# Interleaving the two key/value groups in the compression products of the sparse mixer

## What is computed

```python
HEAD_DIM, NSA_KV_GROUPS, CMP_BLOCK, CMP_STRIDE, CMP_HIDDEN = 64, 4, 32, 16, 128

def compress_blocks(tok, pe, w1, w2):
    seq = tok.shape[1]
    n_cmp = (seq - CMP_BLOCK) // CMP_STRIDE + 1
    idx = np.arange(n_cmp)[:, None] * CMP_STRIDE + np.arange(CMP_BLOCK)[None, :]
    blk = tok[:, idx] + jnp.transpose(pe, (1, 0, 2))[None, None]
    hid = jax.nn.gelu(jnp.einsum('bclgd,gldh->bgch', blk, w1))
    return jnp.einsum('bgch,ghd->bgcd', hid, w2)

def nsa_mixer(...):
    ...
    k_cmp = compress_blocks(rope(kv[:, :, 0]), pe_k, w1_k, w2_k)
    v_cmp = compress_blocks(kv[:, :, 1], pe_v, w1_v, w2_v)
    ...
```

## Time and profile before

| | us |
|---|---|
| median of 3 runs | 4570.61 |
| lowest and highest run | 4568.33, 4572.18 |
| the profiled execution | 4559.27 |
| its span in the profile | 4558.0 |
| PE busy in the span | 4293.0 (94%) |
| the compression, first to last matmul | 2352.80 to 2428.3 |

### The profile page before, as it was taken

How to read it: one execution, slowest core, us unless ns; L and a number is a source line. 1 busy time by engine, 2 the same in 40 slices (tenths; PEclk the granted TensorE clock), 3 DMA queues, 4 the chain that set the end, 5 groups by cost and what they waited for, 6 DMA issues and landing times.

```text
span 4558.0 us, 71840 instructions
## 1 busy us (share of the span) xinstructions
PE 4293.0 (94%) x30760; PEld 3958.4 (87%) x30760; DVE 3061.0 (67%) x4411; ACT 1964.3 (43%) x2499; POOL 117.0 (3%) x112
## 2 busy tenths in 40 slices
PE   7989999999998999979888899999999899999998
PEld 6878888787886888868786899999998799999998
DVE  6667675675767866457535699845955689954864
ACT  4445454454534544445324443243244544234233
POOL 0000000000003000020000000000000000000000
PEclk9989999899999999979975999999999999999999
DMA  5533545254541545415431354354254345345344
GB/s 198 185 108 136 189 176 186 89 185 159 187 163 47 194 176 185 158 46 193 144 114 46 121 182 152 112 185 167 103 186 148 114 173 181 108 159 185 120 158 148
DMA packets 94701, 679.29 MB, mean 149 GB/s; under 512 B 11296, under 2 KB 11952, under 8 KB 12848
## 3 DMA queue, kind: packets, MB, share of 16 engines
q1 hardware_dynamic: 91152, 662.74, 40.5%
q0 software_dynamic: 1024, 7.61, 0.4%
q10 hardware_dynamic: 2208, 4.34, 0.3%
HBM read 671.48 MB, written 3.17 MB: 148 GB/s over the span
## 4 chain that ended last, share of the span: by engine, by line
PE 82%; DVE 14%; ACT 2%; issue 1%; DMA 0%; POOL 0%; ACTq 0%; DVEq 0%; SPq 0%; POOLq 0%
PE psum L625 21%; PE psum L554 15%; PE psum L556 14%; PE psum L555 14%; PE psum L626 10%; PE psum L1185 3%; DVE slab_low L1627 2%; DVE room L2261 1%; DVE room L1898 1%; DVE x L1749 1%; DVE room L2277 1%; DVE room L2259 1%; DVE room L2263 1%; PE psum L576 1%; DVE room L1788 1%
## 5 line engine op out<-in xcount | busy, mean ns | idle before, releaser
L1627 DVE TENSOR_TENSOR slab_low<-slab,slab_high 128x2048 fp32r<-128x2048 f32 x632 | 1448.0, 2291 | 791.0 <-ACT slab_high L1204 788.6
L1204 ACT ACTIVATE slab_high<-slab 128x2048 fp32r<-128x2048 f32 x632 | 1204.0, 1905 | 530.4 <-PE psum L626 258.0
L554 PE MATMUL psum<-h_parts,slab_high 128*128 128x256 f32 x3424 | 994.4, 290 | 66.2 <-DVE h_parts L1672 61.6
L625 PE MATMUL psum<-h_parts,slab_high 128*128 128x512 f32 x2816 | 996.2, 398 | 40.2 <-DVE h_parts L1962 35.5
L555 PE MATMUL psum<-h_parts,slab_high 128*128 128x256 f32 x3424 | 979.7, 286 | 0.0
L556 PE MATMUL psum<-h_parts,slab_low 128*128 128x256 f32 x3424 | 979.1, 286 | 0.0
L626 PE MATMUL psum<-h_parts,slab_low 128*128 128x256 f32 x2816 | 790.6, 281 | 0.0
L554 PEld LDWEIGHTS psum<-h_parts,slab_high 128*128 128x128 f32 x3424 | 667.9, 195 | 79.4 <-issue 70.1
L625 PEld LDWEIGHTS psum<-h_parts,slab_high 128*128 128x128 f32 x2816 | 531.7, 189 | 173.7 <-issue 28.3
L555 PEld LDWEIGHTS psum<-h_parts,slab_high 128*128 128x128 f32 x3424 | 668.5, 195 | 2.0 <-issue 1.9
L556 PEld LDWEIGHTS psum<-h_parts,slab_low 128*128 128x128 f32 x3424 | 667.6, 195 | 0.0
(11 more groups left out here) (291 smaller groups left out, 4766.7 us busy)
## 6 DMA issues: line engine op xcount, KB each, us to landing
slab<-in_up SPq DMA_DIRECT2D x176, 1024.0 KB, 4.8
slab<-in_keys_up SPq DMA_DIRECT2D x128, 1024.0 KB, 4.8
slab<-in_keys_down SPq DMA_DIRECT2D x128, 1024.0 KB, 4.8
slab<-in_down SPq DMA_DIRECT2D x88, 1024.0 KB, 4.8
slab<-in_w_in SPq DMA_DIRECT2D x16, 1024.0 KB, 4.8
slab<-in_wq SPq DMA_DIRECT2D x16, 1024.0 KB, 4.9
slab<-in_w_pw SPq DMA_DIRECT2D x12, 1024.0 KB, 4.8
slab<-in_w_qkv SPq DMA_DIRECT2D x12, 1024.0 KB, 4.8
```

Source lines behind the costliest of these rows:

```text
L554: nc.tensor.matmul(out, lhs[0], rhs[0], start=first, stop=False, **options)
L625: nc.tensor.matmul(out, lhs[0], rhs, start=first, stop=False, **options)
L1204: nc.scalar.activation(k.high[m % PARTS][:, 0:width], k.slabs[m % RING][:, 0:width], ACT.Copy).then_inc(k.rounded.up())
L1627: nc.vector.tensor_tensor(k.low[m % RING][:, 0:width], k.slabs[m % RING][:, 0:width], k.high[m % PARTS][:, 0:width], ALU.subtract).then_in ...
```

## The change

The loop over the two row halves (`gg`) moves from outside the steps to the innermost place: each of the three matmuls of a step is issued for `gg` = 0 and right behind it for `gg` = 1. The same 768 matmuls with the same operands, banks and sums are issued; each bank still gets its 48 terms per slab in the same order. `product` is no longer called here; the matmuls now stand on L1052.

```diff
-                    for gg in range(2):
-                        rows = slice(HD * gg, HD * gg + HD)
-                        out = k.banks[gg][0:NCMP, (2 * a + g) * P:(2 * a + g + 1) * P]
-                        for n in range(16):
-                            cols, at = slice(n * P, (n + 1) * P), 16 * half + n
-                            flat = v.parted_flat[a]
-                            mm = self.product(out, (flat[rows, g, at, 0:NCMP], flat[rows, g, at, NCMP:2 * NCMP]),
-                                              (high[rows, cols], low[rows, cols]), half == 0 and n == 0, half == 1 and n == 15)
+                    for n in range(16):
+                        cols, at = slice(n * P, (n + 1) * P), 16 * half + n
+                        first, last = half == 0 and n == 0, half == 1 and n == 15
+                        flat = v.parted_flat[a]
+
+                        for m, (s, part) in enumerate(((0, high), (0, low), (1, high))):
+                            for gg in range(2):
+                                rows = slice(HD * gg, HD * gg + HD)
+                                mm = nc.tensor.matmul(k.banks[gg][0:NCMP, (2 * a + g) * P:(2 * a + g + 1) * P],
+                                                      flat[rows, g, at, s * NCMP:(s + 1) * NCMP], part[rows, cols],
+                                                      start=first and m == 0, stop=last and m == 2)
                     mm.then_inc(k.slab_done.up())
```

## The result

The changed kernel ran at 4535.74 us in the median of 4 runs (4522.99 to 4543.10), the kernel before at 4569.47 (4566.75 to 4572.18). The ratio is 0.9923 with a 95% interval of 0.9899 to 0.9947: 35 us faster, 24 to 46. The forecast was 4522.3 with a range of 4516 to 4540. The time lies inside, 13 us above the forecast. It also lies within 1 us of the 4536.3 that rival (a), the lower clock throughout, gave; so the time alone does not tell the forecast's case from that rival, and the profile has to.

The account below looks back on a forecast made before the run. PE alone was taken to bound the compression stage (75.5 us at clock 0.50). Pairing, upper clock and slab feed together gave minus 48.3 us: 4559.27 to 4511.0 profiled, 4522.3 with the 11.3 us offset; range 4516 to 4540.

Parts of the forecast that it names:

- rival (a): Compression stage: the clock stays at 0.50, only the pairing counts, minus 34.3 us, 4536.3 us; chance 0.31.
- Pairs side by side: First term, compression matmuls on PE: both row halves overlap throughout, 41.0 us at the lower clock for 75.5, minus 34.3.
- The clock: Second term, compression stage: with all rows fed PE's clock rises to 1.00 at 2358; a slab takes 2.7 us, not 9.4.
- The feed: Slab loads, ACT and DVE limit the faster stage: PE waits 1.5 us for slab 4; L1513 starts 48.3 us sooner.
- rival (d): Upper clock comes, but slab feed is worse or clock falls back: 3 to 8 us less gain; 0.62 including the main case.
- Behind the stage: Copy, gelu, second layer and attention move as one with the stage; attention's clock worth 2 us either way.
- The median: Median of the runs lies 11.3 us above the profiled execution; the same offset turns 4511.0 into 4522.3.
- (b): Overlap at a row-half switch is only a draining store, so nothing changes: 4570 within a few us; chance 0.04.
- (c): Changing row half every matmul empties the array, each costs 305 ns: 159 us more, 4730; chance 0.03.

Follow-up runs that it names:

- strips of 32 rows: Changed kernel with each compression matmul reading only the lower 32 of its 64 rows; 4542.29 us, ratio 0.9931 to the kernel before.
- the block of 12: Row half changes after every 12 matmuls (four steps) instead of after each matmul; run once, 4541.11 us.
- the repeat: The changed kernel again, nothing edited, with more rounds; 4530.72 us in the median of 6 runs, ratio 0.9906 to the kernel before.
- the two kernels with other row counts: Changed kernel with 32 of 64 rows read per matmul (4542.29 us), and with one matmul over all 128 rows per pair (4529.31 us).
- the block of 3: Row half changes after each step of three matmuls instead of after each matmul; 4535.17 us, ratio 0.9911 to the kernel before.
- all rows in one matmul: Changed kernel with one matmul over all 128 rows in place of each pair, 384 in the stage; 4529.31 us, ratio 0.9899 to the kernel before.
- the warm start: Changed kernel with 30 full-size products of no use ahead of the stage, where PE waits; 4523.99 us, ratio 0.9889 to the kernel before.
- the last two kernels: Both on 30 useless products ahead of the stage: ACT's last two roundings and DVE's rests moved later (4523.69 us); 64 more useless products behind the stage (4531.93 us).
- the fillers: Changed kernel with 30 useless products ahead of the stage and 64 more behind it where PE waits; 4531.93 us, ratio 0.9905 to the kernel before.

## Why the prediction was right, point by point

- **Pairs side by side.** Forecast 384 pairs at 107 ns and 34.3 us for this term. Measured alone, with strips of 32 rows, the stage took 41.2 us to the copy, which is 34.3 us less. The reading of the earlier trace rows as a rule was right, and the block of 12 gives its reach, some four matmuls. Two details of it were off without changing the sum: by the line numbers the two streams are 2357.45, .56, .66 and 2357.46, .54, .65, and the last matmul of L1084 at the lower clock took 0.42 us where 0.47 was estimated, which makes 50 ns for one and not 49.
- **The clock.** Forecast a rise at 2358 for a start at 2352.8, by fed rows. It rose 5.0 us after the start (2366.2 for 2361.2), 4.8 in the repeat (2358.2 for 2353.4), and the two kernels with other row counts show that it went by the rows. The choice against rival (a) was the one that mattered for the mechanism; the rows of L1084 and L999 carried it. For the number it mattered little: the range held both cases.
- **The feed.** Forecast 27.2 us from first matmul to copy; it was 30.0 and 29.7. The step that was mis-sized is the sum at the upper clock. A pair takes 60 ns and not 56 (2.9 us a slab, near the upper end of the bounds given), and so does one matmul for all rows, so it is not the pairing that costs the 4 ns; loads take longer when two are in flight, 4.8 to 5.8 us, where 4.8 had been taken as fixed; and there are the pauses for instructions, which the prediction didn't have at all. Slab 9's load began 22.7 us in (forecast 20.4) and ACT took it up at 28.2 (forecast 25.2). The list of DMA issues of the changed kernel has, from 2366 to 2386 us (count, KB, median us to landing):

```profile
slab<-in_w SPq DMA_DIRECT2D x4, 1024.0 KB, 5.2
slab<-in_w_nsa_out SPq DMA_DIRECT2D x2, 1024.0 KB, 5.2
```

  Slab 4's start came out at the time forecast (14.7 us in, measured 14.65), in part by luck. Its rest was ready when the sum had it, but the forecast's wait of 1.5 us for it was not there: a pause for instructions of 1.0 us and the slower pace had used it up (in the repeat PE waited 0.25 us). It is the slabs behind it that lost 3 us, slab 4 itself 1.9 in one pause. That is rival (d), of which the cause was named only in part.
- **Behind the stage.** From the first transpose (L1057, L1060 after) to the last of ACT's sums for the next norm (L1222, L1225 after) the time is 120.4 and 121.3 us in the two profiles before, and 123.6 and 123.7 in those after. The forecast had 2 us either way here. The block of 3 has 123.6 too, but the strips of 32 rows, all rows in one matmul, the block of 12 and the warm start have 122.2, and the last two kernels 121.3 and 121.0. So the change may cost 1 to 3 us here or nothing. In its own two profiles and that of the block of 3, 72 us behind the copy ran at the lower clock, where it was 61 in those of the kernel before.
- **The median.** The sum was made against an execution of 4559.3 us and moved by 11.3 us to the runs shown. That both kernels scatter by 20 us and more outside the stage could not be seen in three runs within 4 us of each other. The forecast gain was 48.3 us; the first comparison showed 35 and the repeat 43, near the 45.5 of the stage less the 1 to 3 us above. How much of the gap in the first comparison was chance can't be told run by run.
- **Rivals.** (b) is refuted by the pace of pairs, which held through the whole stage, above all with the strips; (c) by the same pace; (a) describes the stage of the kernel with strips of 32 rows to the microsecond.

## What to carry to other kernels

Products that use half the rows of the array should alternate between the halves. Here it cost no instruction; switching with every matmul and with every 3 hid one matmul of two, switching with every 12 hid 4.1 of 12, and nothing between was run. The two halves wrote to different PSUM banks in every run, and whether that is needed was not tested. Look at the granted clock of a stage that is "100% busy": matmuls on half the rows kept TensorE at the lower clock for all of 75 us here, and the upper clock was worth 11 of the 45 us. Once a stage runs several times faster, price its suppliers anew: loads in flight together, and the engine's own instructions.

## What the runs showed of the hardware that was not expected

- PE stalled for its own instructions, on a grid of 256 of them, when matmuls went at 30 ns and the DMA engines were 81% busy, up to 1.9 us at a time in the changed kernel and 2.3 with the fillers. At 41 and 53 ns a matmul it did not.
- At a switch of row half, the new half's matmuls started while the old half's last three had not the earlier trace rows: PE did not start its matmuls in the order of the program.
- With a switch every 12 matmuls, a third of them hidden, the clock rose after the same 5 us as with full pairs.
- Two profiles of one kernel differed by 24 us outside of a stage that was equal to 0.01 us; the differences of single executions can't be read as effects of an edit.
